# Block two of a three-block network: input columns in another order, and the convolution, decays and key blocks made under the input products

## What is computed

```
p   = x @ w_in                       # 1024 x 2956: nsa q | six 64-wide keys and values | 12 gates
                                     # | moba q, k, v | conv 2*256 | hgrn q, f, i, g
nsa : keys and values compressed in blocks of 32 tokens (gelu of a product), then three attentions
      of 4 heads x 64: over 15 compressed keys, over selected keys, over a window
moba: one attention of 4 heads x 64
conv: u = a * sigmoid(b);  y[t] = sum_k w[k] * u[t-30+k] + bias   # 31 taps, 256 channels
      y = silu(layer_norm(y)) @ w_pw
hgrn: a linear attention of 4 heads x 64 with a decay exp(cumsum(log sigmoid f)), an rms norm
      of each head, and a gate sigmoid(g)
mix = concat(nsa, moba, conv, hgrn)
x   = layer_norm(2**0.25 * x + mix @ w_out)
```

## Time and profile before

| | us |
|---|---|
| three runs: median (lowest to highest) | 2425.66 (2423.18 to 2427.98) |
| the profiled execution: time | 2420.93 |
| the profiled execution: span | 2419.1 |
| TensorE busy in the span | 2051.0 (85%) |
| VectorE busy | 479.4 (20%) |
| ScalarE busy | 373.3 (15%) |

### The profile page before, as it was taken

How to read it: one execution, slowest core, us unless ns; L and a number is a source line. 1 busy time by engine, 2 the same in 40 slices (tenths; PEclk the granted TensorE clock), 3 DMA queues, 4 the chain that set the end, 5 groups by cost and what they waited for, 6 DMA issues and landing times.

```text
span 2419.1 us, 34577 instructions
## 1 busy us (share of the span) xinstructions
PE 2051.0 (85%) x14185; PEld 1137.5 (47%) x14186; DVE 479.4 (20%) x1057; ACT 373.3 (15%) x831; POOL 321.5 (13%) x149
## 2 busy tenths in 40 slices
PE   6997798668778866998779889999999899888878
PEld 5774222112222211232228665889984546454444
DVE  1043411001111100111110394010211302231111
ACT  1142111011111100111111333100101113120001
POOL 4100212222222122112220000000000000011211
PEclk9998799889889978999989989999999999989999
DMA  9675779999999799997993643555544343359994
GB/s 327 169 249 228 299 300 406 426 426 418 404 427 407 311 426 426 381 401 307 415 392 105 221 174 127 217 165 151 177 146 134 118 131 139 121 213 410 410 408 158
DMA packets 183321, 681.50 MB, mean 282 GB/s; under 512 B 15970, under 2 KB 57219, under 8 KB 150224
## 3 DMA queue, kind: packets, MB, share of 16 engines
q1 hardware_dynamic: 179200, 670.02, 71.0%
q0 software_dynamic: 4032, 10.40, 1.7%
q10 hardware_dynamic: 16, 0.02, 0.0%
HBM read 679.33 MB, written 1.06 MB: 281 GB/s over the span
## 4 chain that ended last, share of the span: by engine, by line
PE 65%; DMA 23%; DVE 6%; ACT 3%; SPq 2%; issue 1%; POOL 0%; DVEq 0%; ACTq 0%; POOLq 0%
PE ps L778 33%; DMA scr<-in_w_mlp 14%; PE ps L1161 8%; PE ps L1187 5%; DMA MOD<-in_w_mlp 4%; PE ps L1486 2%; DMA spare<-in_b_mlp 2%; PE ps L1198 2%; DMA HTY<-in_w 2%; PE ps L815 2%; PE ps L1129 1%; PE ps L1165 1%; PE ps L1523 1%; PE ps L1497 1%; PE ps L861 1%
## 5 line engine op out<-in xcount | busy, mean ns | idle before, releaser
L1161 PE MATMUL ps<-ring,scr 128*32 128x512 f32 x2208 | 300.6, 694 | 131.2 <-POOL ring L724 130.8
L778 PE MATMUL ps<-ring,HTY 128*128 128x512 f32 (+5 forms) x960 | 326.3, 501 | 3.9 <-ACT HTY L1570 3.9
L724 POOL COPY ring<-scr 128x4096 f32<-128x4096 f32 x62 | 223.9, 3617 | 775.3 <-DMA scr<-in_w_mlp 569.1
L778 PEld LDWEIGHTS ps<-ring,HTY 128*128 128x128 f32 x960 | 174.7, 190 | 152.2 <-issue 136.0
L1161 PEld LDWEIGHTS ps<-ring,scr 128*32 128x32 f32 x2208 | 74.1, 122 | 352.3 <-POOL ring L724 179.0
L778 PE MATMUL ps<-HTY,ring 128*128 128x256 f32 (+1 forms) x1072 | 238.0, 385 | 1.7 <-DMA ring<-in_w_ff 1.1
L778 PEld LDWEIGHTS ps<-HTY,ring 128*128 128x128 f32 (+1 forms) x1072 | 205.4, 192 | 32.9 <-ACT HTY L1570 2.4
L2413 DVE TENSOR_SCALAR spare<-ps 128x256 f32<-128x256 f32 x46 | 19.5, 424 | 675.4 <-PE ps L1165 675.4
L1570 ACT ACTIVATE scr<-ps 128x512 f32<-128x512 f32 (+7 forms) x117 | 58.3, 500 | 498.9 <-PE ps L778 403.5
L778 PE MATMUL ps<-ring,scr 128*128 128x128 f32 (+1 forms) x1040 | 121.6, 280 | 1.4 <-DVE scr L2525 1.4
L778 PEld LDWEIGHTS ps<-ring,scr 128*128 128x128 f32 x1040 | 117.5, 192 | 5.2 <-issue 3.3
(11 more groups left out here) (476 smaller groups left out, 1923.3 us busy)
## 6 DMA issues: line engine op xcount, KB each, us to landing
scr<-in_w_mlp SPq DMA_DIRECT2D x94, 2048.0 KB, 25.3
ring<-in_w_mlp SPq DMA_DIRECT2D x34, 2048.0 KB, 20.2
MOD<-in_w_mlp SPq DMA_DIRECT2D x32, 2048.0 KB, 23.8
HTY<-in_w_mlp SPq DMA_DIRECT2D x32, 2048.0 KB, 21.8
ring<-in_w_ada SPq DMA_DIRECT2D x23, 2048.0 KB, 9.2
ring<-in_w_in SPq DMA_DIRECT2D x20, 2048.0 KB, 7.9
ring<-in_w_ff SPq DMA_DIRECT2D x16, 2048.0 KB, 9.5
ring<-in_w SPq DMA_DIRECT2D x16, 2048.0 KB, 16.4
```

Source lines behind the costliest of these rows:

```text
L724: pool.tensor_copy(m1_slabs[j], m1_arrivals[j]).then_inc(moved[j], 1)
L778: mm = pe.matmul(o, lhs(k), rhs(k), start=begin and k == 0, stop=end and k == nk - 1)
L1161: mm = pe.matmul(ps[C1 * c:C1 * (c + 1), 0, :], XG[:, 2 * j + i, :], m1_slabs[j][:, i, BANK * c:BANK * (c + 1)], start=j + i == 0, stop=False)
```

## The change

The part of block two before `out2` is put in another order.

- The slabs of w_in come in the order convolution (1420 to 1932), hgrn q and f (1932 to 2444), then the first 1420 columns in three slabs, then hgrn i and g. The first product of `in2` is made before the wait for the six small loads.
- VectorE starts when the third product of `in2` is read. It does all 60 steps of the convolution, the cumulated decay, its spans and parts, the key blocks, the moments and the norm of the convolution, and the weighing of spans and parts; then it waits for the end of `in2`.
- ScalarE takes the decays' exponentials, the square root and the silu of the convolution between its reads of `in2`.
- TensorE makes the two sets of transposes of the convolution and its product with w_pw inside `in2`, behind waits on `conv_ready` and `convsilu_ready`.
- The tile `LD` lies elsewhere, since its old place is read by `in2`.
- The linear attention's products are made in units 0, 1 and 2, its merging in units 3 and 4, its outputs in unit 5, the head norm in units 6 and 7.
- The mix is turned in halves: the first tokens' attention half in unit 7, the other mixers' half after the last unit, and the second tokens' attention half between the two tiles of `out2`.
- GpSimd's later loads wait for the last unit's output instead of the head norm.

The core of the diff (the rest renames stages in `STAGES` and splits `head_norm` and `turned` in two):

```diff
-            column_slabs(I["w_in_2"][0], [0, 512, 908, 1420, 1932, 2444, 2956])
+            column_slabs(I["w_in_2"][0], [1420, 1932, 2444])
+            column_slabs(I["w_in_2"][0], [0, 512, 908, 1420])
+            column_slabs(I["w_in_2"][0], [2444, 2956])
...
# TensorE, inside in2
+            features([col(w3, 140), col(w3, 268)])
+            pe.wait_ge(conv_ready, 1)
+            b = bank()
+            for a in range(NT):
+                for c in range(2):
+                    mm = pe.transpose(b[:, S * a + P * c:S * a + P * (c + 1)], CACC[:, c, P * a:P * (a + 1)], ident[:, :])
+            close(mm)
...
+            tokens(lambda k: w5[:, k, 0:S], S)
+            pe.wait_ge(convsilu_ready, 1)
...
+            tokens(lambda k: w5[:, k, S:2 * S], S)
+            pe.wait_ge(product_free, silu_read)
+            tokens(lambda k: pww[:, k, :], S, lhs=CSIL, nk=2)
...
# TensorE, between the units
-                if i == 4:
+                if i == 0:
                     linear_diagonal(1)
+                if i == 1:
+                    linear_masked(1)
+                if i == 2:
+                    linear_wide(1)
                 if i == 5:
-                    linear_masked(1)
-                if i == 6:
-                    linear_wide(1)
+                    linear_outputs(1, IH, 64)
                 if i == 7:
-                    turn_convolution()
+                    pe.wait_ge(att["out_read"], n_window + n_nsa // 2)
+                    turn_half(Y, 0, 0)
...
# TensorE, after the units
             pe.wait_ge(mix_ready, 2)
-            turn(Y)
+            pe.wait_ge(product_free, end["in2"])
+            for a in range(NT):
+                turn_half(Y, a, 1)
             pe.wait_ge(product_free, end["mix2T"])
-            wide_by_tile("out2")
+            weights(first_slab["out2"])
+            weights(first_slab["out2"] + 1)
+            for a in range(NT):
+                if a == 1:
+                    pe.wait_ge(att["out_read"], n_window + n_nsa)
+                    turn_half(Y, a, 0)
+                    pe.wait_ge(product_free, done[0])
+                for i in range(2):
+                    w = slot(first_slab["out2"] + i, KT, BANK)
+                    tokens(lambda k: w[:, k, :], BANK, tiles=(a,))
...
# ScalarE, between its reads of in2
+            read(CTOK[:, :, :], two(product()))
+            key_decays()
+            query_decays()
+            part_decays()
             diagonal(product(), 2, 2)
+            root(2)
             read(VM[:, :, :], two(product()))
+            act.wait_ge(convln_ready, 1)
+            act.activation(CTOK[:, :, :], CTOK[:, :, :], ACT.Silu).then_inc(convsilu_ready, 1)
...
# ScalarE, between the units
                 if i == 7:
-                    read(CTOK[:, :, :], two(product()))
+                    turned_half(0, 0)
+                    root(8)
...
# VectorE, under in2
+            dve.wait_ge(product_free, gated_read)
+            tell(dve.tensor_tensor(CA[:, :, CONVW - 1:], CA[:, :, CONVW - 1:], CG[:, :, :], ALU.mult), conv_gated, 1)
...
+            taps(1, 17)
+            log_sigmoid_sums(2, FH, HLOG[:, :, :], HCUM, 1.0)
+            taps(17, CONVW)
+            dve.wait_ge(zeros_again, 2)
+            spans(1, HCUM)
+            parts(1, HCUM)
...
# VectorE, between the units
+                if i == 3:
+                    merge(1, wide_read, (0,))
+                if i == 4:
+                    merge(1, wide_read, (1,))
+                if i == 6:
+                    dve.wait_ge(product_free, outputs_read)
+                    head_squares(1, Y[:, :, 768:], 64)
+                if i == 7:
+                    head_scale(Y[:, :, 768:], GH[:, :, :], 64, 2)
```

More of the change, by code:

```diff
@@ L793, in turn, with turn_half @@
                         close(mm)
+            def turn_half(src, a, half):
+                b = bank()
+                for k in range(4):
+                    mm = pe.transpose(b[:, P * k:P * (k + 1)], src[:, a, P * (4 * half + k):P * (4 * half + k + 1)], ident[:, :])
+                close(mm)
             def tokens(rhs, width, lhs=HT, nk=KT, tiles=range(NT)):
@@ L1235, in _ @@
             turn(X, x1_ready)
+            pe.wait_ge(product_free, end["x1T"])
+            s = first_slab["in2"]
+            weights(s)
+            w = slot(s, KT, BANK)
+            features([col(w, 0), col(w, P)])
             pe.wait_ge(block2_params_landed, 96)
@@ L1253, in _ @@
[L1253 to L1264, removed]
+            features([col(w, S), col(w, S + P)])
@@ L1579, in root, with turned_half @@
                 act.activation(std[:, 0:n], var[:, 0:n], ACT.Sqrt).then_inc(std_ready, 1)
+            def turned_half(a, half):
+                read(HT[:, 4 * half:4 * half + 4, P * a:P * (a + 1)], product().rearrange("p (k n) -> p k n", k=4))
             def turned(tiles=range(NT)):
@@ L1583, in turned @@
                     for half in range(2):
-                        b = product()
-                        read(HT[:, 4 * half:4 * half + 4, P * a:P * (a + 1)], b.rearrange("p (k n) -> p k n", k=4))
+                        turned_half(a, half)
             inputs = [0]
@@ L1886, in _ @@
             row_spread(7)
-            root(2)
-            linear_outputs(Y[:, :, 768:], 64)
-            act.wait_ge(convln_ready, 1)
-            act.activation(CTOK[:, :, :], CTOK[:, :, :], ACT.Silu).then_inc(convsilu_ready, 1)
-            read(CSIL[:, :, :], two(product()))
-            root(8)
-            read(Y[:, :, 512:768], two(product()))
-            turned()
             for a in range(NT):
+                turned_half(a, 1)
+            for a in range(NT):
+                if a == 1:
+                    turned_half(a, 0)
                 for i in range(2):
@@ L2210, in weigh_parts, with merge @@
                     step(ins) if pair == 0 else tell(ins, lin["parts_weighed"], 1)
-            def merge(n, products):
+            def merge(n, products, tiles=range(NT)):
                 dve.wait_ge(product_free, products)
                 tmp = lin_tiles[n]["tmp"]
-                for tile in range(NT):
+                for tile in tiles:
                     a = AT[tile][:, :, 0:P]
@@ L2236, in head_norm, with head_squares @@
             def head_norm(n, o, gate, width, ready):
+                head_squares(n, o, width)
+                head_scale(o, gate, width, ready)
+            def head_squares(n, o, width):
                 squares = lin_tiles[n]["squares"]
@@ L2242, in head_norm, with head_scale @@
                 tell(dve.tensor_scalar(var[:, 0:8], var[:, 0:8], 1.0 / width, 1e-6, ALU.mult, ALU.add), var_ready, roots[0])
+            def head_scale(o, gate, width, ready):
                 dve.wait_ge(std_ready, roots[0])
```

166 lines of the change are left out of this document (74 added, 92 removed).

## The result

The changed kernel takes 2402.64 us (median of four runs, 2401.22 to 2407.1), the kernel before, on the same chip at the same time, 2424.61 (2423.18 to 2427.98). The ratio is 0.9914, with a 95% interval of 0.9897 to 0.993: 0.86% faster by the ratio, 22 us by the medians. The forecast was 2398.2 and a range of 2391 to 2408. The profiled execution took 2401.22, where the working said 2393.5: of 27.4 us that it forecast, 19.7 came.

The account below looks back on a forecast made before the run. VectorE's queue was taken to bound the eight units, while idle in the input products. Terms 3.5 + 13.2 + 12.1 - 1.4 = 27.4 us less, profiled 2393.5; the median, 4.7 higher, 2398.2; range 2391 to 2408.

Parts of the forecast that it names:

- step 6: Tail behind the units 2.0 us instead of 14.1, 12.1 less; its last term, a gap between `out2`'s tiles, 1.4 more.
- Step 1: Start of the input products: first product no longer waits for the small loads, starts 1.3 us sooner.
- Step 2: Input products: transposes and w_pw product add 3.2 us; no wait on VectorE, slack 13 us at convolution, 4 at silu.
- Step 3: Compressed keys: no wait, no cold start, first scores after 10.5 us instead of 11.8.
- Steps 4 and 5: Eight units: TensorE's own queue bounds them, diagonal 2.5 us over that schedule; 76.6 us instead of 89.8, 13.2 less.
- rival A: Clock stays low in several units, 2.9 us more each, 12 in four more; gain 15, time 2411; chance 0.14.
- Step 7: Weight loads: a slab lands 8.7 us after issue, three units last 18 or more; nothing after `out2` waits for a fixed time.
- rival D: Weight slabs come too late in the three shortest units, 5.3 us of waits; gain 22, time 2404; chance 0.07.

Follow-up runs that it names:

- the last experiment: Masked and wide linear sets put before the w_ada matmuls in units 1 and 2, against the kernel with the diagonal in the input products: 2389.03 us, ratio 0.9853.

## Why the prediction was right, and which term was mis-sized

The mechanism stands: `out2` begins at 1450.13 instead of 1477.42, 27.3 us earlier, and steps 1 to 6 up to there forecast 28.8. Then 7.8 us are given back in `out2`, where the sum had 1.4. That term, the last of step 6, is the mis-sized one. Against the forecast, steps 1 to 3 gave 0.9 us more, the units 3.2 less, the tail 0.4 more and `out2` 6.4 less.

Step 1: 1.4 us for 1.3. (x itself was turned 0.37 us earlier, ahead of the change.) Step 2: the stage lasts 95.9 for 96.5, with no wait. The slack at the convolution was 13.0 to 13.2 us for 13. At the silu, which ended at 1344.94 and was asked for at 1349.11, it was 4.2 for 4; that 12.5 us more of steps cost only a wait of 1.20 there is because VectorE had been idle 1.59 and 2.95 us in between and ScalarE's read and table load between the norm and the silu took 2.5 us, all three of which the delay used up (12.5 - 4.5 - 2.5 - 4.2 = 1.3). Step 3: 10.4 for 10.5, without a cold start. Steps 1 to 3 gave 4.4 us for 3.5.

Steps 4 and 5: 79.8 us for 76.6. (TensorE's waits on VectorE before, up to 3.4 us by the rows, reach 3.68 in the trace, which changes nothing in the sum.) The two executions of one program, 77.0 and 81.4 with the tail, lie on both sides of the forecast 78.6. Unit 0 is what differs between them: it was given 14.9 us and took 16.3 and 12.1 (both sets of scores counted). In units 1 and 2 both took more than forecast, 24.5 and 24.4 us for 21.65; from unit 3 to `out2` both took less, 40.6 and 40.5 for 42.05. The forecast had charged low clock to unit 0 alone, and there is also some in units 1 and 2. So a piece of rival A is true, in two units and at 1.4 us each, where it had said 2.9 in four more; the mean clock of the units is 0.85 in both kernels. That units and tail together came out 2.8 us over the forecast and not 1.6 under it is the chance of the execution.

Step 6: the tail took 1.6 for 2.0. The gap of 1.4 was worked out from TensorE's side: a turn, a read and two hand-overs. What was missed is that the reading engine goes through its own program in order, and that the read was written behind a root whose input VectorE makes only from tile 0's last product. The forecast did name this kind of wait in unit 7 (root before copy, 1.36 us in the rows) and not here. Read before root removes it: `out2` 34.2 to 29.0 us, total 6.6 us less. The second part of the loss, 2.9 and 1.7 us in two executions, is the clock at 0.50 and 0.80 behind the idle stretch, which goes with it. The measured time still lay inside its range because the range had room for A, and not for this: as to `out2`, that was luck.

Step 7: no matmul of w_ada has a DMA as its releaser, a slab lands in 9.1 us for 8.7; rival D is out. The stages behind `out2` did not change.

Two rules were weighed in the prediction. ScalarE's rows of the changed kernel:

```profile
1444.05 1.28 ACT L1604 ACT_TABLE_LOAD   x1
1445.34 0.21 ACT L1604 ACTIVATE stat<-stat 128x8 f32<-128x8 f32 x1
1445.46 1.00 ACT L1676 ACTIVATE scr<-ps 128x1024 f32<-128x1024 f32 x1
```

The root begins 1.29 us after the load begins, and the copy right behind it; moved off the path, the pair gave back 1.14 us. The Trainium skill ("ScalarE: Activation LUTs", What ACT_TABLE_LOAD costs) has the load's 1283 ns right, and of its further 1380 ns of drain these rows show none. As to the clock, TensorE was busy 4.00 of 4 us at 1383 to 1387 of the last experiment and was granted 0.50, after 4.00 busy microseconds at 1.00. The Trainium skill ("TensorE: Matmul & The Clock Gate", What's actually happening) says that throttled is the default and that activity releases it. If busy time is meant by activity, this stretch does not agree, as the forecast's row had said.

What stays open is what the clock goes by. The profile models the ends of TensorE's matmuls, so "busy" here means without a recorded gap. Diagonal, masked set and the one-partition rows of unit 2 each had a low stretch on or behind them, but not in every execution and not always of one length: unit 0 lasted 14.6, 10.8 and 13.8 us with the same instructions on TensorE. No run separated the width of the instructions from their kind (weights loaded for each), and none repeated one order of instructions often enough to tell its effect from the chance between executions.

A version that beats both kernels keeps the change and turns the half inside tile 0: 2391.14 us, 1.4% under the kernel before and 9.2 us under the changed one beside it (6.2 of them in `out2`). Root early, diagonal under the inputs and another order in units 1 and 2 (2389.03 to 2393.61) cannot be told from it by total.

## What to carry to other kernels

Work that one engine does too late and that needs only early inputs can be moved under a stage in which that engine is idle; bound it by the slack at every wait for it (here 13.0 us at the first and 4.2 at the second). Up to that slack it cost nothing; beyond it, 18.0 us of waiting made the stage 21.4 us longer. Price a new step on every in-order queue that it passes, also on the engine that only reads its result: what stands before the read, and what does *that* wait for? Charge a pause of TensorE for the clock behind it too: here 1.7 to 2.9 us for one of 4.2 us, 3 us for one of 18.0, nothing for one of 0.74.

## What was not expected of the hardware

- A TensorE without a gap in the profile is granted 0.50 for as long as 6.4 us (1380.60 to 1387.00), on or behind sets of 2- or 64-column matmuls: the same eight instructions of the spread take 1.06 or 1.92 us, the same 64 of the adaptive product 1.95 or 3.02.
- The 32 instructions of the diagonal take 6.99 us behind a wait of 3.43 us, and 4.19 in the same kernel without the wait.
- Unit 0 of one instruction stream lasts 10.8 or 14.6 us from one execution to the next.
- An idle time of 4.18 us of TensorE was followed by 4.2 us at 0.50 and 4 us at 0.80, and cost 2.9 us besides itself; one of 0.74 us cost nothing.
